# Router with its weights' parts stationary and x1 moving, and the gate bias as two float32r products

## The chip, the cores and the metric

One core of one Trainium2 chip. The metric is the device time of one launch in microseconds (us); the kernel before was run three times, and one further execution was profiled. TensorE's clock has two levels, 1.2 and 2.4 GHz; the profile gives the granted clock of a stretch as a share of the higher one.

## The reference, cut to what matters

A hybrid encoder layer with 768 tokens (256 of a prompt, 512 of a sample) and width 1024. After attention and SSD mixing, an output projection and a layer norm give x1. From x1 come two things that the change touches:

```
aff  = softmax(x1 @ w_router)            # 16 experts; per sequence each expert takes its top 32 / 64 tokens
gate, idx = top_k(aff.T, cap)            # 96 tokens per expert in all
moe  = scatter-add over 16 experts of  down(silu(x1[idx] @ w_gate) * (x1[idx] @ w_up)) * gate
ple  = sigmoid(x1 @ w_ple_gate + b_ple_gate) * (p @ w_ple)
y    = layer_norm(ALPHA * x1 + moe + ple)
```

Everything is float32. Sums that must stay exact to float32 are formed from a high and a low part of each operand, rounded to float32r: high x high, high x low, low x high.

## The kernel before, in words

All five engines run a program written out by hand and meet at semaphores. Tokens stand in NT = 6 tiles of 128; D = 1024 is KD = 8 blocks of 128. The stages up to x1 take some 485 us. What follows around the change, with line numbers of the kernel before:

- **x1.** VectorE's x1_norm(t) (L1313) norms tile t and counts s_x1. TensorE's x1_turn(t) (L1779, transposes at L1787) turns it into PSUM; ScalarE's x1_high(t) copies the high part to xT_r, VectorE's x1_low(t) (L1323, L1327) writes the low part to mix_r and counts s_x1T.
- **Gate units.** ple_units are 12 pairs (half h of 512 columns, tile t), h = 0 first. ple_unit(u) (L1791) computes in one PSUM bank: the bias as one f32 product of a row of ones and a bias row (L1800, bias rows in spare space of qksq and dtw, loaded at L504), then 24 float32r products of 512 columns (L1805 to L1807), and in a second bank p @ w_ple as two f32 products (L1811). Each f32 product of 512 columns stands in the trace as two instructions. It counts s_pg. ScalarE's sigmoid(u) (L948) and VectorE's base(u) (L1349, L1350) turn the pair into ALPHA * x1 + ple, which GpSimd writes to acc_rows (L665). Unit u waits for base(u - 2), because the banks alternate.
- **Router.** router(t) (L1815): for tile t, x1's parts are the stationary operand and the router weights move. Eight products of 32 columns (L1818: x1 high with both weight parts), eight of 16 columns (L1820: x1 low with the high part), per tile; 96 in all, into bank 6, with tokens on the partitions. VectorE adds the parts and forms the softmax with one exponential on ScalarE (L1359 to L1367, L976).
- **Search.** TensorE turns the affinities (L1861), VectorE copies them to gB (L1372) and takes the top 32 and 64 tokens in twelve rounds of max, max_index and match_replace (L1379 to L1381) in gB and bB, with base(2), base(3) and base(4) after every fourth round. s_top follows (L1387). TensorE turns the indices (L1868, L1873), and GpSimd gathers rows of x1.
- **TensorE's order** from 476 us: unit 0, x1_turn(5), router of the six tiles, unit 1, affinity turn, units 2 to 5, wait for s_top, index turns, units 6 to 10, turn of expert 0's rows (L1883), unit 11, then the experts: gate_up (L1905) of 384 products and down (L1917) of 384 products each.
- **SyncE's order** (the only queue of weight loads, and a wait there holds all behind it): at s_o NT the first half of expert 0's gate and up weights (load_gu 0 and 1, L512), at s_pg 6 the second half, at s_top the two broadcasts of ln2's gain and bias into gB and bB (L527, L528; 512 KB each in SBUF), at s_pg 12 expert 0's down weights (load_dn, L515), then each expert's weights as the slots come free (s_ug, s_ud).

Of the kernel before, what the change touches and what calls it, by code (L numbers as in the profile page):

```python
# [28 lines left out]
P = 128  # L29
# [36 lines left out]
def hymba_layer(nc, A, consts, out_prompt, out_sample):  # L66
# [16 lines left out]
    with ctx:  # L83
        def sb(name, shape, dt=F32):
            return ctx.enter_context(nc.sbuf_tensor(name, shape, dt))

        def sem(name):
            return ctx.enter_context(nc.semaphore(name))
# [8 lines left out]
        def over(name, base, skip, shape):  # L97
            return nc.alloc_sbuf_tensor_at(name, shape, F32R, offset=at[base] + 4 * skip).ap()
# [14 lines left out]
        ones = sb("ones", [P, P])  # L113
# [70 lines left out]
        bple = [qksq[0:1, 0:512], dtw[0:1, 0:6, :].rearrange("p r c -> p (r c)")[:, 0:512]]  # L184

# [31 lines left out]
        wr2 = over("wr2", "dtw", 512, [P, KD, 2 * NE])  # L217
# [121 lines left out]
        s_bple = sem("s_bple")  # L339
        s_bn = sem("s_bn")  # L340
# [48 lines left out]
        def gate_bank(u):  # L389
            return 2 * (u % 2)  # L390
# [42 lines left out]
        def _(sp):  # L433
# [69 lines left out]
            for h in range(2):  # L503
                sp.dma_start(bple[h], A["b_ple_gate"][:, h * 512:(h + 1) * 512]).then_inc(s_bple, 16)  # L504
# [212 lines left out]
        def _(act):  # L717
# [7 lines left out]
            def copy(o, i):  # L725
                return nc.scalar.activation(o, i, ACT.Copy)  # L726
# [210 lines left out]
            copy(wr2[:, :, 0:NE], wr[:]).then_inc(s_wrh, 1)  # L937
# [72 lines left out]
        def _(dve):  # L1010
# [300 lines left out]
            nc.vector.tensor_tensor(wr2[:, :, NE:2 * NE], wr[:], wr2[:, :, 0:NE], ALU.subtract).then_inc(s_wrl, 1)  # L1311
# [179 lines left out]
        def _(pe):  # L1491
# [299 lines left out]
            def ple_unit(u):  # L1791
                h, t = ple_units[u]
                if u == 0:
                    pe.wait_ge(s_x1T, NT - 1)
                    pe.wait_ge(s_bple, 32)
                    pe.wait_ge(s_wple, 16)
                if u >= 2:
                    pe.wait_ge(s_base, u - 1)
                b, c = gate_bank(u), p_bank(u)
                nc.tensor.matmul(ps[:, b, :], ones[0:1, :], bple[h], start=True, stop=False)  # L1800
                for k in range(KD):
                    if t == 0 and k % 4 == 0:
                        pe.wait_ge(s_wpl, 2 * h + k // 4 + 1)
                    x_h, x_l = xT_r[:, k, t * P:(t + 1) * P], mix_r[:, t, k * P:(k + 1) * P]
                    nc.tensor.matmul(ps[:, b, :], x_h, wpg_h[h][:, k, :], start=False, stop=False)  # L1805
                    nc.tensor.matmul(ps[:, b, :], x_h, wpg_l[h][:, k, :], start=False, stop=False)  # L1806
                    nc.tensor.matmul(ps[:, b, :], x_l, wpg_h[h][:, k, :], start=False, stop=(k == KD - 1))  # L1807
                if u == 2 * NT - 1:
                    pe.wait_ge(s_base, u)
                for k in range(2):  # L1810
                    last = nc.tensor.matmul(ps[:, c, :], pT[:, k, t * P:(t + 1) * P],  # L1811
                                            wple[:, k, h * 512:(h + 1) * 512], start=(k == 0), stop=(k == 1))
                last.then_inc(s_pg, 1)

            def router(t):  # L1815
                o = ps[:, 6, 2 * NE * t:2 * NE * (t + 1)]
# [47 lines left out]
            for u in range(2, 6):  # L1864
                ple_unit(u)
# [118 lines left out]
```

## Time and profile before

| | us |
|---|---|
| median of 3 runs | 1182.03 (1181.91 to 1183.86) |
| the profiled execution, its own time | 1182.11 |
| its span, first to last instruction | 1180.3 |
| TensorE busy | 1072.2 (91% of the span) |
| VectorE, ScalarE, GpSimd busy | 439.7, 253.0, 287.5 |
| mean granted clock of TensorE | 0.960 |
| moved by DMA | 254.01 MB, 215 GB/s over the span |

The time of the execution is 1.8 us above its span. Busy time of TensorE contains products that wait in its pipeline, so the distance between starts tells the price of a product, not its length. Times of rows count from the start of the span. A bracket at the end of a row of a timeline is the idle time before it and what ended that.

### The profile page before, as it was taken

To read this page: it belongs to the slowest core of one execution; us is meant where nothing else is said; L and a number is where in the kernel's file an instruction comes from. 1 tells how busy PE (TensorE), PEld (TensorE's weight loads), DVE (VectorE), ACT (ScalarE), POOL (GpSimd) and SP (SyncE) were. 2 spreads that over 40 slices of the span, in tenths; PEclk is the share of its full clock that TensorE was granted. 3 is DMA by queue.
4 is the path that set the end of the run, shared out by engine and by line. 5 is a ranking of instruction groups with operands and counts; after the bars stand their busy time and mean duration, and the time that the engine had idled before them with its cause. 6 is when DMAs were issued, how large, how long until landed. Compare 5 with 4: busy or idle time off the path is not lost.

```text
span 1180.3 us, 20730 instructions
## 1 busy us (share of the span) xinstructions
PE 1072.2 (91%) x8811; PEld 611.9 (52%) x8811; DVE 439.7 (37%) x870; ACT 253.0 (21%) x530; POOL 287.5 (24%) x311
## 2 busy tenths in 40 slices
PE   5999778888998899999999999999999999999940
PEld 3568666665655587866643344444443344444420
DVE  5436785457678867656100011111011011111018
ACT  1143334256656621300011000000000000000002
POOL 0006994234545100000100122211122122210134
PEclk9999988979999999789999999999999999999985
DMA  9010200300000620404269999999999999999854
GB/s 337 14 61 11 72 1 1 98 10 0 2 1 1 211 101 36 187 18 158 97 252 406 385 385 386 398 396 386 388 397 392 390 388 387 397 393 404 320 166 176
DMA packets 63119, 254.01 MB, mean 215 GB/s; under 512 B 7384, under 2 KB 15448, under 8 KB 46688
## 3 DMA queue, kind: packets, MB, share of 16 engines
q1 hardware_dynamic: 52544, 234.48, 50.9%
q0 software_dynamic: 10528, 18.88, 6.5%
q8 instruction: 32, 0.52, 0.2%
q14 instruction: 15, 0.12, 0.0%
HBM read 237.62 MB, written 15.73 MB: 215 GB/s over the span
## 4 chain that ended last, share of the span: by engine, by line
PE 72%; DVE 11%; DMA 7%; POOL 6%; ACT 2%; issue 2%; SPq 0%; DVEq 0%; POOLq 0%; ACTq 0%
PE ps L1905 25%; PE ps L1917 12%; PE ps L1563 4%; DMA ring<-in_w_e_up 2%; DMA late<-in_w_e_down 2%; PE ps L1669 2%; PE ps L1684 2%; PE ps L1805 2%; PE ps L1557 2%; PE ps L1807 2%; PE ps L1806 2%; PE ps L1811 2%; PE ps L1883 1%; PE ps L1774 1%; PE ps L1775 1%
## 5 line engine op out<-in xcount | busy, mean ns | idle before, releaser
L1905 PE MATMUL ps<-ring,mix 128*32 128x512 f32 x1536 | 170.7, 592 | 1.1 <-DMA ring<-in_w_e_up 1.1
L1905 PE MATMUL ps<-late,mix 128*32 128x512 f32 x1536 | 171.1, 593 | 0.0
L1408 DVE TENSOR_TENSOR mix<-mix,ps 128x768 f32<-128x768 f32 x16 | 15.3, 954 | 321.6 <-ACT mix L988 321.6
L988 ACT ACTIVATE mix<-ps 128x768 f32<-128x768 f32 x16 | 13.0, 811 | 478.8 <-PE ps L1905 478.8
L1905 PEld LDWEIGHTS ps<-ring,mix 128*32 128x32 f32 x1536 | 49.7, 110 | 116.5 <-issue 113.4
L1905 PEld LDWEIGHTS ps<-late,mix 128*32 128x32 f32 x1536 | 48.2, 110 | 108.7 <-issue 107.8
L1917 PE MATMUL ps<-late,mix 128*32 128x256 f32 x1536 | 86.2, 380 | 2.9 <-DVE mix L1402 2.5
L1917 PE MATMUL ps<-ring,mix 128*32 128x256 f32 x1536 | 85.9, 379 | 1.4 <-DMA ring<-in_w_e_down 1.4
L1415 DVE TENSOR_SCALAR mix<-ps,att 128x256 f32<-128x256 f32 x48 | 20.3, 477 | 162.0 <-PE ps L1917 162.0
L681 POOL DMA_INDIRECT acc_rows<-mix,idx_now x48 | 74.9, 1561 | 20.5 <-POOL idx_now L689 10.7
L1917 PEld LDWEIGHTS ps<-ring,mix 128*32 128x32 f32 x1536 | 49.7, 110 | 34.6 <-DMA ring<-in_w_e_down 1.9
L1917 PEld LDWEIGHTS ps<-late,mix 128*32 128x32 f32 x1536 | 48.9, 110 | 35.2 <-DVE mix L1402 3.0
L686 POOL COPY idx_now<-idxT 96x1 int32 (+1 forms) x14 | 2.5, 181 | 219.2 <-PE ps L1883 219.2
L689 POOL COPY idx_now<-idx 128x3 int32 (+1 forms) x16 | 3.0, 186 | 195.3 <-DVE mix L1415 195.3
L1646 PE MATMUL ps<-xT 128*128 128x512 f32 (+1 forms) x96 | 45.0, 555 | 1.3 <-issue 1.3
L1563 PE MATMUL ps<-ring,xT 128*128 128x512 f32 x96 | 44.9, 623 | 1.2 <-ACT xT L726 1.2
L1537 PE MATMUL ps<-xl,wh 128*128 128x512 f32 (+1 forms) x128 | 44.0, 344 | 0.0
L850 ACT ACTIVATE ring<-ps,att 128x512 f32<-128x512 f32 (+1 forms) x48 | 29.3, 611 | 49.0 <-DVE att L1182 48.8
L1091 DVE SCALAR_TENSOR_TENSOR late<-late,cw 128x770 f32<-128x770 f32 x32 | 39.1, 1226 | 0.9
L1805 PE MATMUL ps<-ring_r,xT_r 128*128 128x512 f32 x96 | 39.3, 409 | 0.0
L1660 PE MATMUL ps<-cst,ring 128*128 128x128 f32 x160 | 27.9, 291 | 11.4 <-DVE gb_in L1190 5.4
L1806 PE MATMUL ps<-late_r,xT_r 128*128 128x512 f32 x96 | 37.9, 395 | 0.0
(289 smaller groups left out, 1812.4 us busy)
## 6 DMA issues: line engine op xcount, KB each, us to landing
late<-in_w_e_gate SPq DMA_DIRECT2D x32, 1024.0 KB, 18.0
late<-in_w_e_up SPq DMA_DIRECT2D x32, 1024.0 KB, 20.0
ring<-in_w_e_gate SPq DMA_DIRECT2D x32, 1024.0 KB, 17.0
ring<-in_w_e_up SPq DMA_DIRECT2D x32, 1024.0 KB, 20.0
late<-in_w_e_down SPq DMA_DIRECT2D x16, 2048.0 KB
ring<-in_w_e_down SPq DMA_DIRECT2D x16, 2048.0 KB
ring<-in_w_in SPq DMA_DIRECT2D x3, 2048.0 KB, 9.0
late<-in_w_ple_gate SPq DMA_DIRECT2D x2, 2048.0 KB, 14.1
```

What stands on the lines that cost most here:

```text
L681: pool.indirect_dma_start(acc_quarters, bass.IndirectOffsetOnAxis(ap=idx_now[:, 1 + i:2 + i], axis=0), ye[:, i, :], None, compute_op=ALU.a ...
L850: nc.scalar.activation(prob[:, u % 4, 0:L], ps[:, u % 3, 0:L], ACT.Exp, bias=att[:, 0, u:u + 1], scale=HD ** -0.5, accum_out=att[:, 1, u:u ...
L1091: ins = nc.vector.scalar_tensor_tensor(conv[:, m, :], u_pad[:, m, j:j + CW], cw[:, m, j:j + 1], conv[:, m, :], ALU.mult, ALU.add)
L1537: nc.tensor.matmul(o, w_h, xl[:, k, a * P:(a + w) * P], start=False, stop=False)
L1557: last = nc.tensor.matmul(bank[:, 0:272], lhs[k], wkv[:, k, :], start=(k == 0), stop=(k == KD - 1))
L1563: last = nc.tensor.matmul(bank, lhs[k], slotk[0][:, k, :], start=(k == 0), stop=(k == KD - 1))
L1646: nc.tensor.matmul(ps[:, u % 3, 0:n * P], qT[:, h % 4, t * P:(t + 1) * P], kz[:, h // 4, a * P:(a + n) * P], start=True, stop=True).then_i ...
L1660: last = nc.tensor.transpose(ps[:, 3, b * P:(b + 1) * P], prob[:, u % 4, b * P:(b + 1) * P], ident)
L1805: nc.tensor.matmul(ps[:, b, :], x_h, wpg_h[h][:, k, :], start=False, stop=False)
L1806: nc.tensor.matmul(ps[:, b, :], x_h, wpg_l[h][:, k, :], start=False, stop=False)
L1905: last = nc.tensor.matmul(ps[32 * j:32 * (j + 1), GU + g, :].rearrange("p (w c) -> p w c", w=2), xeT[:, k, 32 * g:32 * (g + 1)], gu_w[q][: ...
L1917: last = nc.tensor.matmul(ps[32 * j:32 * (j + 1), DN + g, 0:256], src[:, k, 32 * g:32 * (g + 1)], dn_w[d][:, i, 256 * j:256 * (j + 1)], st ...
```

## The change

- The router becomes router(t0, t1, bank): the stationary operand is a 96-column slice of wr2 (block k's high and low parts in its first 32 columns; what follows them is other blocks' or padding, and its output is not read), and x1's high and low parts move, 512 columns for tiles 0 to 3 and 256 columns for tiles 4 and 5. 32 products instead of 96; the logits come with experts on the partitions.
- ScalarE copies the 32 rows of logits to SBUF (gB), TensorE turns them back per tile (six transposes into bank 4), and VectorE reads them as before.
- The bias row is loaded once to partition 32 of gB, split into a high part (ScalarE, into bB) and a low part (VectorE, in place), and added by two float32r products with a row of ones, behind the 24 products instead of ahead of them.
- ple_unit is cut into ple_gate and ple_rest. New order on TensorE: gate of unit 0, x1_turn(5), router in two parts, rest of unit 0, gate of unit 1, logits' turn, rest of unit 1, unit 2, affinity turn, units 3 to 5, wait for s_top and on as before.
- SyncE loads the bias after the last x1 norm; the down weights of expert 0 go ahead of ln2's broadcasts, which now stand behind s_pg 12.

```diff
@@ SyncE
-            for h in range(2):
-                sp.dma_start(bple[h], A["b_ple_gate"][:, h * 512:(h + 1) * 512]).then_inc(s_bple, 16)
...
             load_gu(0, 0)
             load_gu(0, 1)
+            sp.wait_ge(s_x1, NT)
+            sp.dma_start(bple_raw, A["b_ple_gate"]).then_inc(s_bple, 16)
             sp.wait_ge(s_pg, NT)
             load_gu(0, 2)
             load_gu(0, 3)
+            sp.wait_ge(s_pg, 2 * NT)
+            load_dn(0, 0)
+            load_dn(0, 1)
             sp.wait_ge(s_top, 1)
             sp.dma_start(gB[:], bc(A["ln2_g"][0])).then_inc(s_ln2, 16)
             sp.dma_start(bB[:], bc(A["ln2_b"][0])).then_inc(s_ln2, 16)
-            sp.wait_ge(s_pg, 2 * NT)
-            load_dn(0, 0)
-            load_dn(0, 1)
@@ ScalarE
-            copy(wr2[:, :, 0:NE], wr[:]).then_inc(s_wrh, 1)
+            copy(wr2k[:, :, 0, :], wr[:])
+            copy(wr2[:, KD * 2 * NE:], wr[:, 0:4, :].rearrange("p k e -> p (k e)")).then_inc(s_wrh, 1)
...
+            act.wait_ge(s_bple, 16)
+            copy(bple_h, bple_raw).then_inc(s_bplh, 1)
+            act.wait_ge(s_lg, 1)
+            copy(logitsT[:, 0:512], ps[0:2 * NE, 6, :])
+            copy(logitsT[:, 512:T], ps[0:2 * NE, 7, 0:T - 512]).then_inc(s_lgT, 1)
             sigmoid(0)
             wpg_high(1, 0)
             wpg_high(1, 1)
@@ VectorE
+            nc.vector.tensor_copy(ones_r, ones[:])
...
+            dve.wait_ge(s_bplh, 1)
+            nc.vector.tensor_tensor(bple_l, bple_raw, bple_h, ALU.subtract).then_inc(s_bpll, 1)
             base(0)
             wpg_low(1, 0)
             wpg_low(1, 1)
-            dve.wait_ge(s_lg, 1)
-            lg2 = ps[:, 6, 0:NT * 2 * NE].rearrange("p (t w e) -> p t w e", t=NT, w=2)
+            dve.wait_ge(s_lg, 2)
+            lg2 = ps[:, 4, 0:NT * 2 * NE].rearrange("p (t w e) -> p t w e", t=NT, w=2)
@@ TensorE
+            def ple_rest(u):
+                h, t = ple_units[u]
+                if u == 0:
+                    pe.wait_ge(s_bpll, 1)
+                    pe.wait_ge(s_wple, 16)
+                c = slice(h * 512, (h + 1) * 512)
+                nc.tensor.matmul(ps[:, gate_bank(u), :], ones_r[32:33, :], bple_h[:, c], start=False, stop=False)
+                nc.tensor.matmul(ps[:, gate_bank(u), :], ones_r[32:33, :], bple_l[:, c], start=False, stop=True)
...
+            def router(t0, t1, bank):
+                o = ps[0:CAP, bank, 0:(t1 - t0) * P]
                 for k in range(KD):
-                    last = nc.tensor.matmul(o, xT_r[:, k, t * P:(t + 1) * P], wr2[:, k, :], start=(k == 0), stop=False)
-                for k in range(KD):
-                    last = nc.tensor.matmul(o[:, 0:NE], mix_r[:, t, k * P:(k + 1) * P], wr2[:, k, 0:NE], start=False,
-                                            stop=(k == KD - 1))
-                if t == NT - 1:
+                    w = wr2[:, 2 * NE * k:2 * NE * k + CAP]
+                    nc.tensor.matmul(o, w, xT_r[:, k, t0 * P:t1 * P], start=(k == 0), stop=False)
+                    last = nc.tensor.matmul(o, w, mix_r[:, t0:t1, k * P:(k + 1) * P], start=False, stop=(k == KD - 1))
+                if t1 == NT:
                     last.then_inc(s_lg, 1)
...
-            ple_unit(0)
+            ple_gate(0)
             x1_turn(NT - 1)
             pe.wait_ge(s_wrl, 1)
+            router(0, 4, 6)
+            pe.wait_ge(s_x1T, NT)
+            router(4, NT, 7)
+            ple_rest(0)
+            ple_gate(1)
+            pe.wait_ge(s_lgT, 1)
             for t in range(NT):
-                pe.wait_ge(s_x1T, t + 1)
-                router(t)
-            ple_unit(1)
+                last = nc.tensor.transpose(ps[:, 4, t * 2 * NE:(t + 1) * 2 * NE], logitsT[:, t * P:(t + 1) * P],
+                                           ident[0:2 * NE, 0:2 * NE])
+            last.then_inc(s_lg, 1)
+            ple_rest(1)
+            ple_unit(2)
...
-            for u in range(2, 6):
+            for u in range(3, 6):
                 ple_unit(u)
```

## Rows read from the trace of the kernel before

**Rows 1.** Windows, one expert: us, busy of each engine (instructions), PEclk, DMA share, GB/s
```profile
691.00:724.00 33.00, 33.00 (x399) 13.80 (x398) 3.05 (x7) 1.68 (x3) 5.99 (x6) 1.00 1.03 392
```
**Rows 2.** Line 512, loads issued at 606 to 630 us, then at 1020 to 1050 us
```profile
DMA to landing us min/median/max: 11.9/13.7/15.8
...
DMA to landing us min/median/max: 21.3/24.6/28.4
```
**Rows 3.** Timeline of PE, 549 to 602 us: start us, duration us, instruction
```profile
549.16 0.22 PE L1868 MATMUL ps<-cst 16*96 16x16 f32 x1
...
549.83 1.12 PE L1800 MATMUL ps<-dtw,ones 1*128 1x512 f32 x2
...
591.92 1.02 PE L1883 MATMUL ps<-cst,mix 96*128 96x96 f32 x8
...
601.30 1.92 PE L1905 MATMUL ps<-late,mix 128*32 128x512 f32 x16
```
**Rows 4.** Timeline of PE, 476 to 523 us
```profile
476.23 1.12 PE L1800 MATMUL ps<-qksq,ones 1*128 1x512 f32 x2
...
485.01 1.09 PE L1787 MATMUL ps<-cst,xa 128*128 128x128 f32 x8 [0.28 <-DVE xa L1030]
485.86 1.04 PE L1818 MATMUL ps<-wr,xT_r 128*128 128x32 f32 x8
486.75 1.04 PE L1820 MATMUL ps<-wr,mix_r 128*128 128x16 f32 x8
...
504.06 2.07 PE L1800 MATMUL ps<-qksq,ones 1*128 1x512 f32 x2
...
514.68 0.82 PE L1861 MATMUL ps<-cst,rt 128*16 128x128 f32 x6
515.42 1.12 PE L1800 MATMUL ps<-qksq,ones 1*128 1x512 f32 x2
516.48 0.50 PE L1805 MATMUL ps<-ring_r,xT_r 128*128 128x512 f32 x1
...
522.05 1.88 PE L1811 MATMUL ps<-gb_in,kvd 128*128 128x512 f32 x4
```
**Rows 5.** Windows around the fall and the rise of the clock (columns as rows 1)
```profile
488.00:490.00 2.00, 2.00 (x14) 2.00 (x13) 1.34 (x3) 1.99 (x3) 0.00 (x0) 0.61 0.58 229
...
508.00:510.00 2.00, 2.00 (x8) 1.61 (x7) 0.00 (x0) 0.00 (x0) 0.00 (x0) 0.77 0.00 0
```
**Rows 6.** Line 512, the four loads issued at 476.3 to 479.1 us
```profile
DMA to landing us min/median/max: 9.9/10.7/11.6
```
**Rows 7.** Timeline of VectorE and ScalarE, 483 to 488 us
```profile
483.73 1.22 DVE L1030 TENSOR_TENSOR xa<-xa,bB 128x1024 f32<-128x1024 f32 x1
...
486.14 1.08 ACT L726 ACTIVATE xT_r<-ps 128x512 fp32r<-128x512 f32 x2 [4.75 <-PE ps L1787]
```
**Rows 8.** Timeline of VectorE, 516 to 547 us
```profile
516.84 0.94 DVE L1372 COPY gB<-ps 16x768 f32<-16x768 f32 x1
...
524.66 0.69 DVE L1349 TENSOR_TENSOR ssdw<-ssdw,ps 128x512 f32<-128x512 f32 x1 [1.47 <-ACT ssdw L948]
...
546.17 0.18 DVE L1387 TENSOR_SCALAR cst<-cst 16x64 f32<-16x64 f32 x1
```
**Rows 9.** Windows with idle time of PE, and after (columns as rows 1)
```profile
156.00:160.00 4.00, 0.99 (x8) 0.86 (x8) 3.69 (x5) 3.29 (x6) 3.84 (x4) 1.00 0.00 0
168.00:171.00 3.00, 1.28 (x6) 1.12 (x7) 2.96 (x3) 2.95 (x6) 2.92 (x3) 1.00 0.00 0
171.00:175.00 4.00, 3.03 (x8) 1.82 (x6) 3.93 (x5) 1.21 (x1) 3.84 (x4) 0.57 0.00 0
```
**Rows 10.** Line 527, issued at 551.3 us, and windows near it (columns as rows 1)
```profile
DMA to landing us min/median/max: 13.3/13.3/13.3
...
560.00:564.00 4.00, 4.00 (x20) 3.28 (x19) 0.80 (x4) 0.00 (x0) 0.54 (x1) 1.00 1.00 326
564.00:568.00 4.00, 4.00 (x12) 1.85 (x11) 0.56 (x1) 0.60 (x1) 0.00 (x0) 1.00 0.42 166
```

More of the change, by code:

```diff
@@ L112, in hymba_layer @@
         hpar = sb("hpar", [P, 3, 16])
-        ones = sb("ones", [P, P])
+        ones = sb_at("ones", [P, P])
         wr = sb("wr", [P, KD, NE])
@@ L216, in hymba_layer @@
         wpg_raw, wpg_h, wpg_l = [slotk[4], slotk[5]], [ring_r[1], ring_r[2]], [late_r[1], late_r[2]]
-        wr2 = over("wr2", "dtw", 512, [P, KD, 2 * NE])
+        wr2 = over("wr2", "dtw", 0, [P, KD * 2 * NE + 2 * 32])
+        wr2k = wr2[:, 0:KD * 2 * NE].rearrange("p (k w e) -> p k w e", k=KD, w=2)
+        logitsT = gB[0:2 * NE, 0:T]
+        ones_r = over("ones_r", "ones", 0, [P, P])
+        gB_r, bB_r = over("gB_r", "gB", 0, [P, D]), over("bB_r", "bB", 0, [P, D])
+        bple_raw, bple_h, bple_l = gB[32:33, :], bB_r[32:33, :], gB_r[32:33, :]
         HALF_K = [slice(0, 4), slice(4, 8)]
@@ L339, in hymba_layer @@
         s_bple = sem("s_bple")
+        s_bplh = sem("s_bplh")
+        s_bpll = sem("s_bpll")
+        s_lgT = sem("s_lgT")
         s_bn = sem("s_bn")
@@ L1310, in _ @@
             dve.wait_ge(s_wrh, 1)
[L1311 removed]
+            nc.vector.tensor_copy(ones_r, ones[:])
+            nc.vector.tensor_tensor(wr2k[:, :, 1, :], wr[:], wr2k[:, :, 0, :], ALU.subtract).then_inc(s_wrl, 1)
             def x1_norm(t):
@@ L1789, in x1_turn, with ple_gate @@
                 last.then_inc(s_tr, 1)
-            def ple_unit(u):
+            def ple_gate(u):
                 h, t = ple_units[u]
@@ L1794, in ple_unit @@
                     pe.wait_ge(s_x1T, NT - 1)
-                    pe.wait_ge(s_bple, 32)
-                    pe.wait_ge(s_wple, 16)
                 if u >= 2:
                     pe.wait_ge(s_base, u - 1)
-                b, c = gate_bank(u), p_bank(u)
-                nc.tensor.matmul(ps[:, b, :], ones[0:1, :], bple[h], start=True, stop=False)
                 for k in range(KD):
@@ L1803, in ple_unit @@
                         pe.wait_ge(s_wpl, 2 * h + k // 4 + 1)
+                    o = ps[:, gate_bank(u), :]
                     x_h, x_l = xT_r[:, k, t * P:(t + 1) * P], mix_r[:, t, k * P:(k + 1) * P]
-                    nc.tensor.matmul(ps[:, b, :], x_h, wpg_h[h][:, k, :], start=False, stop=False)
-                    nc.tensor.matmul(ps[:, b, :], x_h, wpg_l[h][:, k, :], start=False, stop=False)
-                    nc.tensor.matmul(ps[:, b, :], x_l, wpg_h[h][:, k, :], start=False, stop=(k == KD - 1))
+                    nc.tensor.matmul(o, x_h, wpg_h[h][:, k, :], start=(k == 0), stop=False)
+                    nc.tensor.matmul(o, x_h, wpg_l[h][:, k, :], start=False, stop=False)
+                    nc.tensor.matmul(o, x_l, wpg_h[h][:, k, :], start=False, stop=False)
+            def ple_rest(u):
[6 more added lines that the diff above has]
+                nc.tensor.matmul(ps[:, gate_bank(u), :], ones_r[32:33, :], bple_l[:, c], start=False, stop=True)
                 if u == 2 * NT - 1:
@@ L1810, in ple_unit @@
                 for k in range(2):
-                    last = nc.tensor.matmul(ps[:, c, :], pT[:, k, t * P:(t + 1) * P],
-                                            wple[:, k, h * 512:(h + 1) * 512], start=(k == 0), stop=(k == 1))
+                    last = nc.tensor.matmul(ps[:, p_bank(u), :], pT[:, k, t * P:(t + 1) * P],
+                                            wple[:, k, c], start=(k == 0), stop=(k == 1))
                 last.then_inc(s_pg, 1)
-            def router(t):
-                o = ps[:, 6, 2 * NE * t:2 * NE * (t + 1)]
-                for k in range(KD):
-                    last = nc.tensor.matmul(o, xT_r[:, k, t * P:(t + 1) * P], wr2[:, k, :], start=(k == 0), stop=False)
-                for k in range(KD):
-                    last = nc.tensor.matmul(o[:, 0:NE], mix_r[:, t, k * P:(k + 1) * P], wr2[:, k, 0:NE], start=False,
-                                            stop=(k == KD - 1))
-                if t == NT - 1:
+            def ple_unit(u):
+                ple_gate(u)
+                ple_rest(u)
+            def router(t0, t1, bank):
+                o = ps[0:CAP, bank, 0:(t1 - t0) * P]
+                for k in range(KD):
+                    w = wr2[:, 2 * NE * k:2 * NE * k + CAP]
+                    nc.tensor.matmul(o, w, xT_r[:, k, t0 * P:t1 * P], start=(k == 0), stop=False)
+                    last = nc.tensor.matmul(o, w, mix_r[:, t0:t1, k * P:(k + 1) * P], start=False, stop=(k == KD - 1))
+                if t1 == NT:
                     last.then_inc(s_lg, 1)
```

1 line of the change is left out of this document (removed).

## The prediction, made before the changed kernel was run

> **What bounds the kernel now.** I read the windows of the expert stage first: TensorE is busy in all of the 33 us that one expert takes, and the DMA engines show a share of 1.03 [rows 1]. Two resources are full, so I asked which one falls behind. The time from issue to landing of the expert loads answers that: median 13.7 us for loads issued at 606 to 630 us, 24.6 us at 1020 to 1050 us [rows 2]. The queue grows by some 11 us over 13 experts, so transfers are slightly slower than matmuls. From the first down load at about 601 us on the end is therefore fixed by "start of this stage plus bytes to move". That start hangs on TensorE: SyncE waits for s_pg 12, the end of gate unit 11, and the first expert matmul follows at 601.30 us [rows 3].
>
> So the question is what the change does to TensorE's path from 476 to 601 us, and then what it adds to the DMA queue behind it. TensorE has no gap of note there [rows 3, 4]; its clock has: it falls within 488 to 490 us (mean 0.61) and rises within 508 to 510 us (0.77), so the stretch between, 20.5 us, runs at 1.2 instead of 2.4 GHz [rows 5].
>
> **Up to the affinity turn.** The old router starts at 485.86 and ends at 504.06 us: 96 products in 18.2 us. At full clock eight took 0.89 us, 0.11 each [rows 4], whatever their 16 or 32 columns; at half clock twice that. Unit 1 follows, 10.6 us because half of it is at half clock, then the turn of the affinities (0.74 us) until 515.42 us. That is 29.6 us from router start to turn end.
>
> The new order over the same stretch, at full clock, with 24 products of a gate unit taking 5.57 us, 0.232 each [rows 4]:
> - Router part 1, 16 products of 512 columns: 3.7 us. Part 2, 16 of 256 columns: half the price, 0.116, just over the 0.11 that a new stationary operand costs: 1.9 us. Ends 491.5 us. The Trainium skill, "TensorE: Matmul & The Clock Gate", section "Back-to-back issue gap", gives about 131 ns for a 512-column product in a stream of weight loads and products, and 216 ns isolated. By the first, part 1 would take 2.1 us and the sum would be 1.6 us lower; by this trace's 0.232 us in just such a stream the second is nearer, and I give the first no weight.
> - The rest of unit 0: the two bias products. The f32 bias costs 1.06 us now [rows 4]; no row shows two float32r products of one row. Bounds: twice 0.232 = 0.46 us, or no saving. I take 0.56 (0.46 and a little for the switch of rows), so 0.5 us saved per unit: it is the same instruction kind as the gate's. The P products cost 1.80 us (8.43 for a unit, less 1.06 and 5.57). Together 2.4 us.
> - It must wait for the bias's low part. The bias row is issued after the last x1 norm, whose gap ends at 485.01 us [rows 4], behind four expert loads that land 9.9 to 11.6 us after their issue at 476 to 479 us, the last near 489.0 [rows 6]. Then a copy of 1x1024 on ScalarE (two of 512 columns took 1.08 us) and a subtraction on VectorE (1.22 us) [rows 7]: 491.8 us with hand-overs. TensorE waits some 0.3 us. On ScalarE the logit copies and sigmoid 0 queue behind that copy, on VectorE base 0 and the low parts of the second half's weights; the softmax then ends near 504, while TensorE works until 511. Nobody waits.
> - Gate of unit 1 5.6 us, six turns of the logits 0.74 (as the affinity turn), rest of unit 1 2.4, **unit 2, moved ahead**, 7.9, affinity turn 0.74.
> Sum 25.8 us: the turn ends at 511.7 instead of 515.4 us, 3.7 us earlier although it now has unit 2 ahead of it.
>
> **From the turn to the experts.** Now: 515.42 to 601.30 us, 85.9 us [rows 3, 4]. Units 2 to 5 take 8.43 us each (33.7 us to 549.16) and cover the top-k search. That search runs on VectorE from 516.84 to 546.35 us with 1.47 us of waiting in it, 28.0 us of work with three base steps [rows 8]. It is done 2.8 us before TensorE asks.
> After: only units 3 to 5 are left as cover, 3 x 7.93 = 23.8 us. The search needs 0.3 us of hand-over and 28.0 us of work from the turn's end, so **TensorE now stalls 4.5 us**, part of it ahead of unit 5 (which needs base 3) and the rest at s_top. Then 0.67 us of index turns, units 6 to 10 at 7.93 (39.65; now 42.09), the turn of expert 0's rows 0.95, unit 11 7.93: 77.5 us. Saved: 8.4 us. Together 12.1 us at full clock.
>
> **The clock** takes some back. Without bias and P products, unit 0's gate ends at 481.8 us, 3.2 us ahead of x1; now this gap is 0.28 us [rows 4]. Rows on both sides: 3.01 us idle of the 4 us from 156 us left the clock at 1.00; 1.72 us idle of the 3 us from 168 us were followed by about 3.4 us at half (0.57 over 171 to 175 us) [rows 9]. So it may or may not fall; I think it mostly does, and dense 512-column products then bring it back sooner than the old router did. I take 5 us at half clock, 2.5 us lost (bounds 0 and half of 20.5 us). The stall at s_top with the tiny index products behind it can do the same ahead of unit 6; a fall ahead of unit 5 instead would be covered by the search. I take 1.0 us, between 0 (clock stays, or the search covers it) and 3.4 (7 us at half).
>
> **The DMA queue.** The bias's two old loads of 2 KB, on an idle queue, cost nothing. The two 512 KB broadcasts of ln2 move from an idle queue at 551 us to behind the first down loads, ahead of every load of expert 1. They are then in the stage that the queue bounds, and the price is their time on the queue. By bytes, 1.05 MB at the stage's 392 GB/s [rows 1] are 2.7 us; at the 326 GB/s that a full queue (share 1.00) moved from 560 to 564 us, while they were in it, 3.2 us [rows 10]. The upper end is their landing time of 13.3 us [rows 10]. I take 3.1, near the row in which they ran themselves. Nothing hides it: TensorE's own slack against the queue is used up by the end of the stage.
>
> The other edits (a copy of ones on VectorE, a small second copy of router weights on ScalarE) come before the output products end, while both engines wait for TensorE, and cost nothing; without that cover they would be some 0.5 us.
>
> **Sum**: -12.1 + 2.5 + 1.0 + 3.1 = -5.5 us against the profiled execution's own 1182.11 us (span 1180.3), which stands 0.08 us above the median: 1176.6 us.
>
> **The rivals.**
> A. The clock stays up in both new gaps, as in the first of those rows: -9.0 us, 1173.1; with the bias at its cheap bound and ln2 at 2.7 us, 1171.5. For it: the search has units between its two waits. Against: the second of those rows, where less idle time was enough.
> B. The clock falls at the new gap and stays down through the second router part, bias waits and turns, as it did for 20.5 us, some 15 us, and once more at s_top: 8 to 9 us lost, about 1181. This needs unit 1's dense products not to end it early; now they did, within that unit [rows 5]. A costly bias product ends in the same place: no saving in 8 units on the path is 4 us, 1180.6.
> C. **Slower**: the ln2 broadcasts, all reading one 4 KB row 128 times, hold the queue for most of their 13.3 us landing time when they stand ahead of expert 1. At 13.3 us instead of 3.1 the time is 1186.8. It decides from about 11 us on (3.1 + 5.5 + 2.4). Against: the share of 0.42 over 564 to 568 us shows the queue empty soon after [rows 10].
> D. The change doesn't do what it says: the wide router products run as full f32 (0.90 us for a P product) instead of at the gate's price. The tiles are float32r views as in the gate, so I hold it for unlikely; with 0.9 and 0.45 us per product the router costs 21.6 us, 1192.
>
> **How the numbers follow.** Forecast 0.48, A 0.20, B 0.20, C 0.07, D 0.05. A measurement of this kernel tells about 0.2%, 2.4 us, from no change: faster means below 1179.7. The forecast's own range is 1174 to 1180, nearly all faster; B lies mostly within the bound; C and D are slower, but for part of B that spills over. Faster 0.72, same 0.17, slower 0.11. The range takes in A's low bound and B: 1171.5 to 1182.0; above it lie C and D.
>
> **What would show it.** In the profile after: router products in two groups of about 3.7 and 1.9 us (up to twice that at half clock); a gap of about 3 us ahead of 485 us; gate units at 7.9 us; an idle TensorE ahead of unit 5 and ahead of the index turns, 4 to 5 us together, released by VectorE; first expert matmul near 592.7 us (589 with the clock up); landing of expert 1's first loads some 3 us longer. Wrong would be: a unit still at 8.4 us, no stall at s_top, the first expert matmul after 597 us, or a stage from there to the end that differs from 580 us by other than the ln2 loads' 3 us.

## The result, and the profile after

The changed kernel takes **1174.45 us** (median of 4 runs, 1173.55 to 1174.80) against 1181.97 us before (4 runs beside it): the ratio is 0.9935, 95% interval 0.9919 to 0.9951. It is faster by 7.5 us (0.65%); 5.5 us were forecast. A second measurement, beside 11 runs of the kernel before, gave 1174.14 us and 0.9932 [0.9916, 0.9949].

The profiled execution took 1173.55 us, its span 1171.6 us; so it is 0.9 us under the median, and 8.6 us under the profiled execution of the kernel before. Line numbers below are those of the changed kernel. First the timeline of TensorE after the change, answering to [rows 4]:

```profile
485.19 1.71 PE L1798 MATMUL ps<-cst,xa 128*128 128x128 f32 x8 [3.11 <-DVE xa L1038]
486.55 0.78 PE L1840 MATMUL ps<-xT_r,wr 128*96 128x512 f32 x1
...
491.43 0.28 PE L1840 MATMUL ps<-xT_r,wr 128*96 128x256 f32 x1
...
493.41 0.50 PE L1823 MATMUL ps<-bB_r,ones_r 1*128 1x512 f32 x1
493.75 0.39 PE L1824 MATMUL ps<-gB_r,ones_r 1*128 1x512 f32 x1
494.07 1.99 PE L1828 MATMUL ps<-gb_in,kvd 128*128 128x512 f32 x4
...
501.60 0.50 PE L1823 MATMUL ps<-bB_r,ones_r 1*128 1x512 f32 x1
...
512.14 0.82 PE L1889 MATMUL ps<-cst,rt 128*16 128x128 f32 x6
```

The gap of 0.28 us ahead of x1's last turn has become 3.11 us. The router's first part takes 4.88 us (486.55 to 491.43), its second 1.98 us: 6.9 us instead of 18.2. The two bias products take 0.66 us together (493.41 to 494.07) instead of 1.06. From the bias of unit 0 to the bias of unit 1 it is 8.19 us (493.41 to 501.60), with the six turns of the logits in it. Bias and P products end the unit, and six turns of the affinities start at 512.14 us, 2.5 us earlier than before, although unit 2 now stands ahead of them.

The clock (columns as in [rows 1]), answering to [rows 5]:

```profile
484.00:486.00 2.00, 0.81 (x5) 0.81 (x6) 1.13 (x1) 0.00 (x0) 0.53 (x1) 0.88 1.00 422
486.00:488.00 2.00, 2.00 (x9) 1.56 (x8) 0.00 (x0) 1.06 (x2) 0.00 (x0) 0.50 1.02 418
488.00:490.00 2.00, 2.00 (x8) 1.39 (x7) 1.63 (x3) 1.09 (x2) 0.00 (x0) 0.77 0.63 252
490.00:492.00 2.00, 2.00 (x12) 1.53 (x11) 0.87 (x1) 0.00 (x0) 0.00 (x0) 1.00 0.05 20
```

It falls right behind the gap and is back within 488 to 490 us. By the means (0.12, 0.50 and 0.23 short of 1.00, over 2 us each, doubled) that is 3.4 us at half clock, where it was 20.5 us.

The search and what follows it, answering to [rows 3] and [rows 8], on TensorE and then on VectorE:

```profile
530.80 0.50 PE L1813 MATMUL ps<-ring_r,xT_r 128*128 128x512 f32 x1 [1.62 <-DVE cst L1359]
541.13 0.22 PE L1896 MATMUL ps<-cst 16*96 16x16 f32 x1 [2.03 <-DVE cst L1398]
547.49 0.50 PE L1823 MATMUL ps<-bB_r,ones_r 1*128 1x512 f32 x1
...
555.53 0.50 PE L1823 MATMUL ps<-bB_r,ones_r 1*128 1x512 f32 x1
...
582.14 1.02 PE L1911 MATMUL ps<-cst,mix 96*128 96x96 f32 x8
...
591.18 1.06 PE L1933 MATMUL ps<-late,mix 128*32 128x512 f32 x8
```
```profile
512.99 0.94 DVE L1383 COPY gB<-ps 16x768 f32<-16x768 f32 x1 [5.12 <-PE ps L1889]
...
540.90 0.18 DVE L1398 TENSOR_SCALAR cst<-cst 16x64 f32<-16x64 f32 x1
```

TensorE now stalls for 1.62 us ahead of unit 5 (released by base 3) and 2.03 us at s_top: 3.65 us, both released by VectorE, whose search runs 28.1 us without a wait. A gate unit takes 8.04 us (547.49 to 555.53) instead of 8.43. The first expert matmul comes at 591.18 instead of 601.30 us.

In the expert stage, windows of the same 33 us, then the landing times of loads of line 512 issued at 595 to 620 and at 1010 to 1040 us, answering to [rows 1, 2]:

```profile
691.00:724.00 33.00, 33.00 (x402) 13.88 (x398) 3.15 (x6) 1.68 (x3) 6.00 (x6) 1.00 1.03 395
```
```profile
DMA to landing us min/median/max: 14.3/16.1/18.0
...
DMA to landing us min/median/max: 21.0/24.3/27.9
```

Loads of expert 1 land after 16.1 instead of 13.7 us: the two broadcasts stand ahead of them. How the stage keeps its pace shows in the turns of an expert's rows (L1911), one per expert, and in TensorE's waits from 950 to 1075 us:

```profile
933.68 1.13 PE L1911 MATMUL ps<-cst,mix 96*128 96x96 f32 x8
966.78 1.13 PE L1911 MATMUL ps<-cst,mix 96*128 96x96 f32 x8
1000.62 1.13 PE L1911 MATMUL ps<-cst,mix 96*128 96x96 f32 x8
1034.95 1.13 PE L1911 MATMUL ps<-cst,mix 96*128 96x96 f32 x8
```
```profile
PE ps L1933 <- DMA ring<-in_w_e_up: 2.1, 3, 1.0
```

From the third turn up to 966.78 us an expert takes 33.10 us, before the change and after it: there TensorE sets the pace, while the queue falls behind. Only the last experts wait for their up weights, three times and 2.1 us in all; two of them show here with 33.84 and 34.33 us.

**A ruler.** Across the 13 profiles of this study the start of the last operation of x1's norm lies anywhere from 482.09 to 484.65 us, though nothing ahead of it was changed on purpose but small copies. TensorE's clock early in the execution goes with it. The windows of 120 to 300 us in the profiles of e3, of the changed kernel and of e8, in which that operation starts at 482.56, 483.91 and 484.65 us:

```profile
120.00:300.00 180.00, 144.66 (x704) 111.14 (x703) 115.59 (x241) 83.46 (x198) 101.12 (x115) 0.92 0.09 30
...
120.00:300.00 180.00, 147.41 (x706) 113.34 (x704) 114.90 (x238) 82.72 (x194) 100.60 (x115) 0.91 0.10 30
...
120.00:300.00 180.00, 148.72 (x705) 115.05 (x704) 114.74 (x237) 82.84 (x194) 100.74 (x114) 0.90 0.09 30
```

The four profiles with a mean clock of 0.92 there (e1, e3, e6, e10) have the operation at 482.1 to 482.8 us; of the eight with 0.91, six have it at 483.7 to 484.6 us, and e7 and e5 at 484.31 and 482.36 us. The medians move likewise: of the six runs of e11, the changed kernel again, two with a mean clock of 0.970 and 0.971 over the whole execution took 1171.9 us, four with 0.965 and 0.966 took 1174.1 to 1174.9 us. So medians of 4 to 6 runs can differ by up to 2 us without an edit. What makes the clock fall more or less often in those early stages stays open.

So I compare two stretches: from that start to the index turns (the path of router, gates and search), and from the index turns to the last expert matmul (gates 6 to 11 and the experts).

| kernel | x1 to index turns | index turns to last matmul | median, us |
|---|---|---|---|
| before | 65.43 | 587.7 | 1181.97 |
| changed | 57.22 | 586.8 | 1174.45 |
| changed, again | 57.24 | 587.2 | 1174.14 |

The first stretch repeats to 0.02 us, the second to half a us. The change gains 8.2 us in the first and, with cheaper gates against the ln2 loads, 0.5 to 0.9 us in the second. That goes with the 8.6 us between the two profiled executions; the medians differ by 7.5 us.

### The profile page after: what moved, and what is told of

Its sections match the earlier page's. It is cut to its first block, busy times and chain, and to the rows that moved or that the text cites. A ratio compares the mean times of both kernels' runs of the same rounds, so it can differ in the third digit from the quotient of the medians.

```text
span 1171.6 us, 20620 instructions
## 1 busy us (share of the span) xinstructions
PE 1057.4 (90%) x8753; PEld 600.2 (51%) x8753; DVE 441.1 (38%) x872; ACT 255.4 (22%) x534; POOL 287.7 (25%) x311
## 4 chain that ended last, share of the span: by engine, by line
PE 67%; DVE 13%; DMA 9%; POOL 6%; issue 2%; ACT 2%; SPq 0%; DVEq 0%; POOLq 0%; ACTq 0%
PE ps L1933 24%; PE ps L1945 11%; DMA ring<-in_w_e_up 7%; PE ps L1574 4%; PE ps L1680 2%; PE ps L1695 2%; PE ps L1568 2%; PE ps L1828 1%; PE ps L1785 1%; PE ps L1787 1%; PE ps L1786 1%; PE ps L1813 1%; PE ps L1814 1%; PE ps L1815 1%; DVE xT L1467 1%
## 5 line engine op out<-in xcount | busy, mean ns | idle before, releaser
L1419 DVE TENSOR_TENSOR mix<-mix,ps 128x768 f32<-128x768 f32 x16 | 15.3, 954 | 323.0 <-ACT mix L996 323.0
L683 POOL DMA_INDIRECT acc_rows<-mix,idx_now x48 | 75.0, 1562 | 20.5 <-POOL idx_now L691 10.7
```

Of the source, the lines that this page charges most:

```text
L683: pool.indirect_dma_start(acc_quarters, bass.IndirectOffsetOnAxis(ap=idx_now[:, 1 + i:2 + i], axis=0), ye[:, i, :], None, compute_op=ALU.a ...
```

## The experiments

Each is the changed kernel with the edit shown. Its ratio is to the kernel before, measured beside it. "Under" and "above the changed kernel" compare with its first median, 1174.45 us, where nothing else is said, and carry the uncertainty of up to 2 us told above; the first stretch is free of it.

**e1: the f32 bias back.**

```diff
-nc.tensor.matmul(..., ones_r[32:33, :], bple_h[:, c], start=False, stop=False)
-nc.tensor.matmul(..., ones_r[32:33, :], bple_l[:, c], start=False, stop=True)
+nc.tensor.matmul(..., ones[32:33, :], bple_raw[:, c], start=False, stop=True)
```

> The changed kernel with one part undone: the gate bias is again one f32 product of a row of ones and the bias row (still behind the 24 gate products, still loaded after the last x1 norm); the copy to a high part on ScalarE and the subtraction on VectorE are gone. Theory (TensorE's path sets the start of the expert stage, and units 3 to 5 are hidden by the search): the bias costs about 1.05 us per unit instead of 0.66 us, 0.39 us more. Of twelve units nine are on the path (units 0 to 2 and 6 to 11), so the first expert matmul comes at 591.2 + 3.5 = 594.7 us and the time is 1174.45 + 3.5 = 1178.0 us; the two stalls of the search shrink from 3.65 to about 2.5 us together. Rival (the bias is paid in all twelve units, the search hides nothing): +4.7 us, 1179.1. Rival (the float32r form saves nothing at this width): 1174.5.

Measured: 1177.29 us (0.9958 [0.9942, 0.9975]), 2.8 us above the changed kernel, between the three expectations and nearest to the first; its four runs (1176.1 to 1178.9 us) don't separate the first from the second, the waits below do. Its units and its clock behind the index turns, from the timeline and the windows:

```profile
549.18 1.12 PE L1818 MATMUL ps<-gB,ones 1*128 1x512 f32 x2
...
557.63 1.12 PE L1818 MATMUL ps<-gB,ones 1*128 1x512 f32 x2
```
```profile
542.00:546.00 4.00, 4.00 (x11) 3.13 (x12) 0.50 (x1) 0.00 (x0) 0.54 (x1) 0.57 0.99 393
```

A unit costs 8.45 us again, 0.4 us more than with float32r products, and the first stretch is 58.42 us, 1.20 us longer: three units' bias, as only units 0 to 2 stand ahead of the search. The waits shrink from 3.65 to 2.56 us, so units 3 to 5 are indeed covered. In this profile the clock fell behind the wait at s_top (0.57 over 542 to 546 us, 3.4 us at half); in the changed kernel's own two profiles it did not. It is the slowest of the four runs, 1178.86 us.

**e2: the old router back**, with unit 2 still ahead of the affinity turn.

```diff
-router(0, 4, 6)
-pe.wait_ge(s_x1T, NT)
-router(4, NT, 7)
+for t in range(NT):
+    pe.wait_ge(s_x1T, t + 1)
+    router(t)
...
-act.wait_ge(s_lg, 1)
-copy(logitsT[:, 0:512], ps[0:2 * NE, 6, :])
-copy(logitsT[:, 512:T], ps[0:2 * NE, 7, 0:T - 512]).then_inc(s_lgT, 1)
...
-    last = nc.tensor.transpose(ps[:, 4, t * 2 * NE:(t + 1) * 2 * NE], logitsT[:, t * P:(t + 1) * P],
```

router(t) and wr2 have their old form again, and VectorE reads the logits from bank 6.

> The changed kernel with the other part undone: the router as before the change (x1's parts stationary, 96 products per run of six tiles, logits with tokens on the partitions, no copy of logits and no turn back), in the place where the new router stands; the bias as two float32r products, unit 2 ahead of the affinity turn, and ln2's loads behind the down loads stay. Theory (the router was dear because of its 96 changes of the stationary operand and because the clock fell under it): router 17 to 19 us instead of 6.9 us, unit 1's first part at half clock again, less 0.2 us of logit turn; first expert matmul at 601 to 604 us, time 1185 to 1187 us, slower than the kernel before, since the search's stall and the ln2 loads are still paid. Rival (the half clock came from the old order and its f32 bias, not from the router's small products): the router costs 10.8 us at full clock, +4 us, 1178.5.

Measured: 1189.71 us (1.0067 [1.0050, 1.0083]), 15.3 us above the changed kernel and 3 us more than the theory's upper end. From its timeline, the start of the router and of the bias behind it, then its windows:

```profile
487.04 1.87 PE L1836 MATMUL ps<-wr,xT_r 128*128 128x32 f32 x8
...
507.60 0.79 PE L1819 MATMUL ps<-bB_r,ones_r 1*128 1x512 f32 x1
```
```profile
486.00:488.00 2.00, 2.00 (x12) 2.00 (x10) 0.00 (x0) 0.58 (x2) 0.20 (x1) 0.50 1.05 436
...
512.00:514.00 2.00, 2.00 (x8) 1.36 (x7) 0.77 (x2) 1.41 (x2) 0.00 (x0) 0.80 0.00 0
```

Here the clock is down when the router starts, behind the gap (3.15 us), and stays down through it and into the next gate, from 485.5 to 512.8 us: 27.3 us instead of the 20.5 us before the change. The router's 96 products take 20.6 us, all at half clock. In this order the new router is worth more than the whole change. The miss of the theory is that it took the old router at its old price, of which the first part ran at full clock, and the old length of half clock with it.

**e8: the bias part alone**, e2 and in addition unit 2 behind the affinity turn, as before the change; against e2:

```diff
 ple_rest(1)
-ple_unit(2)
...
-for u in range(3, 6):
+for u in range(2, 6):
```

> Of the change only the bias part and what it forces: old router in its old form and unit 2 behind the affinity turn as before, bias as two float32r products behind the gate's, ln2's broadcasts behind the down loads. Theory (the float32r bias saves 0.39 us per unit on TensorE, 4.7 us, while the gap ahead of 485 us costs 3.1 us, the half clock that begins in it and lasts through the router 3 to 4 us more, and ln2's loads 3.5 us): slower than the kernel before, 1185 to 1187 us. Rival (the bias part pays for itself): 1179 to 1181 us.

Measured: 1184.94 us (1.0033 [1.0021, 1.0044]): slower than before, at the lower end of what was expected. Split off from the router, the bias part loses: its row must wait for x1's gain and bias rows to be free, which opens the gap, costs clock under the old router, and pushes the ln2 loads into the expert stage. The 4.7 us that it saves on products by the theory don't pay that; the parts were not measured one by one here. e5 below has the order of e8 with the new router, 1169.20 us: with unit 2 behind the affinity turn the router is worth 15.7 us, with unit 2 ahead of it 15.3 us (e2).

**e3: the ln2 loads behind the last down load.**

```diff
-sp.wait_ge(s_top, 1)
-sp.dma_start(gB[:], bc(A["ln2_g"][0])).then_inc(s_ln2, 16)
-sp.dma_start(bB[:], bc(A["ln2_b"][0])).then_inc(s_ln2, 16)
...
     load_dn(NE - 1, d)
+sp.wait_ge(s_top, 1)
+sp.dma_start(gB[:], bc(A["ln2_g"][0])).then_inc(s_ln2, 16)
+sp.dma_start(bB[:], bc(A["ln2_b"][0])).then_inc(s_ln2, 16)
```

> The changed kernel with ln2's two broadcasts issued after the last down load of the expert stage instead of ahead of expert 1's loads; nothing else. Theory (the DMA queue bounds the expert stage, so 1 MB ahead of it costs its time on the queue): 2.5 to 3.2 us faster, 1171.5 us. Rival (TensorE bounds most of the stage, and the stage's end hangs on the last down load's own latency): within 0.8 us of 1174.45. Second rival (the late loads then delay the closing layer norm, which waits for them): slower than 1174.45 by up to 10 us.

Measured: 1170.90 us (0.9914 [0.9898, 0.9931]), 3.5 us under the changed kernel and 3.2 us under its second measurement. Landing of line 512's loads issued at 596 to 620 us, and TensorE's waits from 950 to 1075 us:

```profile
DMA to landing us min/median/max: 10.2/13.5/15.8
```
```profile
PE ps L1933 <- DMA ring<-in_w_e_up: 0.8, 1, 0.8
```

Median 13.5 instead of 16.1 us, and 0.8 instead of 2.1 us of waits. The first stretch is unchanged (57.26 us), the second 583.5 instead of 587 us. No wait of the closing norm for the late loads stands in the profile. The steadiest measure runs from the first expert matmul to the end of the span: 578.2, 578.0 and 577.4 us in the three profiles with late loads (e3, e7, e10) against 580.3 to 580.8 us in seven with early ones (the changed kernel twice, e2, e5, e6, e8, e9; e1 has 581.8). The broadcasts cost 2.7 us between the means, 2.1 to 3.4 us between single profiles.

So both theories were right in part. TensorE sets the pace of most experts, as the rival said; but the queue never makes up for the megabyte, and the last experts pay for it.

**e4: the ln2 loads twice.**

```diff
 sp.dma_start(bB[:], bc(A["ln2_b"][0])).then_inc(s_ln2, 16)
+sp.wait_ge(s_ln2, 32)
+sp.dma_start(gB[:], bc(A["ln2_g"][0])).then_inc(s_ln2, 16)
+sp.dma_start(bB[:], bc(A["ln2_b"][0])).then_inc(s_ln2, 16)
```

> The changed kernel with ln2's two broadcasts issued a second time, when the first pair has landed, still early in the expert stage (1 MB more on the queue, nobody computes with it); SyncE waits for the first pair to land before that, which also holds back the loads of expert 1 behind it. Theory (queue bound): +3 us for the megabyte and up to some us more for the loads held back, 1178 us or above. Rival (TensorE bound): the queue has room, within 0.8 us of 1174.45.

Measured: 1180.99 us (0.9996 [0.9982, 1.0009]), 6.5 us above the changed kernel, with ten runs from 1178.65 to 1184.68 us. Slow enough for the theory, but for another reason: the hold of SyncE. Expert 1's loads leave at 610.6 instead of 596.6 us, and TensorE waits for them, with the clock at half behind that wait:

```profile
622.23 6.98 PE L1936 MATMUL ps<-late,mix 128*32 128x512 f32 x48 [7.17 <-DMA late<-in_w_e_up]
```
```profile
618.00:626.00 8.00, 3.77 (x20) 1.04 (x24) 0.00 (x0) 0.00 (x0) 0.00 (x0) 0.57 1.01 365
```

By the mean of 0.57 the clock is at half for some 6.9 us. The wait and half of that are 10.6 us; the stage of this profile is 590.2 us, 9.8 us longer than the changed kernel's. So nothing is left that would be the second megabyte's, and e4 can't tell a price per megabyte. That rests on e3, e7 and e10.

**e5: unit 2 behind the affinity turn.**

```diff
 ple_rest(1)
-ple_unit(2)
...
-for u in range(3, 6):
+for u in range(2, 6):
```

> The changed kernel with unit 2 moved back behind the affinity turn, as before the change. Theory (the search of 28.3 us needs four gate units of 8.04 us as cover, and has three): TensorE waits about 1 us for the softmax ahead of the affinity turn, the turn ends near 506 us instead of 513, units 2 to 5 run to 538.3 us without a wait ahead of unit 5 or at s_top, so the index turns begin 2.8 us earlier than the 541.1 us of the changed kernel, and the time is 1171.7 us. Rival (the 3.65 us of waiting there are not on the path, the DMA queue is): 1174.45 us, no change. Rival (the softmax comes so late that unit 2 ahead of the turn was needed): slower than 1174.45.

Measured: 1169.20 us (0.9899 [0.9883, 0.9916]). Its timeline of TensorE, with VectorE's last norm operation at 482.36 us:

```profile
503.59 0.82 PE L1888 MATMUL ps<-cst,rt 128*16 128x128 f32 x6 [1.12 <-DVE rt L1378]
...
536.53 0.22 PE L1895 MATMUL ps<-cst 16*96 16x16 f32 x1
```

A wait of 1.12 us for the softmax, none at s_top: 54.17 us for the first stretch, 3.05 us less than the changed kernel, as expected. The median moved by 5.2 us. The second stretch (587.3 us) doesn't hold the other 2 us. The early x1 does in the profiles: 1169.03 against 1173.55 us are 4.5 us, of which 3.05 lie in the first stretch and 1.55 ahead of it (482.36 against 483.91 us). The mean clock of its four runs is 0.968 and 0.969, that of the changed kernel's four 0.965 to 0.967.

**e6: the gap filled.**

```diff
 ple_gate(0)
-x1_turn(NT - 1)
 pe.wait_ge(s_wrl, 1)
+pe.wait_ge(s_res, NT)
 router(0, 4, 6)
+x1_turn(NT - 1)
+ple_gate(1)
 pe.wait_ge(s_x1T, NT)
 router(4, NT, 7)
 ple_rest(0)
-ple_gate(1)
```

> The changed kernel with router part 1 (tiles 0 to 3) ahead of x1's last turn and the gate of unit 1 behind that turn, ahead of router part 2, so that TensorE has work in the gap of 3.1 us ahead of 485 us and while tile 5's parts are copied. Unit 2 stays whole ahead of the affinity turn. Theory (gap and the half clock that it brings lie on the path): 3.1 us of gap and 1.7 us of half clock go, the affinity turn comes 4.3 to 4.8 us earlier, the search with its waits moves along, first expert matmul at 586.6 us, time 1169.9 us; no fall of the clock near 485 us. Rival (the bias row or the softmax on VectorE ends last then, since their times don't move): 1.5 to 2.5 us gained only, 1172.3.

Measured: 1170.07 us (0.9911 [0.9895, 0.9928]). Timeline of TensorE, x1's last norm operation at 482.09 us:

```profile
483.78 1.03 PE L1798 MATMUL ps<-cst,xa 128*128 128x128 f32 x8
...
505.33 0.82 PE L1890 MATMUL ps<-cst,rt 128*16 128x128 f32 x6
...
534.59 0.22 PE L1897 MATMUL ps<-cst 16*96 16x16 f32 x1 [2.03 <-DVE cst L1398]
```
```profile
476.00:1110.00 634.00, 623.97 (x6632) 287.39 (x6630) 104.41 (x206) 47.71 (x74) 94.31 (x103) 1.00 0.89 341
```

No gap, and the granted clock does not fall from 476 us up to the tail of the expert stage at 1110 us. The first stretch is 52.50 us, 4.72 us less: the theory's 4.3 to 4.8.

**e9: fillers in the gap.** Twelve float32r products of 512 columns, whose result nobody reads, ahead of x1's last turn.

```diff
 ple_gate(0)
+pe.wait_ge(s_wrl, 1)
+pe.wait_ge(s_res, NT)
+for k in range(12):
+    nc.tensor.matmul(ps[0:CAP, 7, :], wr2[:, 0:CAP], xT_r[:, k % KD, 0:512], start=True, stop=True)
 x1_turn(NT - 1)
```

> The changed kernel with 12 float32r products of 512 columns, whose result nobody reads, in the gap of 3.1 us ahead of x1's last turn; all that is read is computed as before. Theory (the clock falls because of the gap, and half a clock for 3.4 us costs 1.7 us of path): no fall of the clock near 485 us, the path from the start of x1's last norm operation to the index turns 55.5 instead of 57.2 us, time 1.7 us less than the changed kernel. Rival (the turn of 128x128 blocks or the following waits bring the fall, not the gap): the clock falls all the same, no gain. Second rival (the fillers delay the turn): up to 1 us slower.

Measured: 1172.24 us (0.9913 [0.9895, 0.9931]), 1.9 us under the second measurement of the changed kernel, made beside it. Its windows and, from its timeline, x1's last turn and the index turns (x1's last norm operation: 484.46 us):

```profile
540.00:544.00 4.00, 3.93 (x57) 3.23 (x58) 1.30 (x3) 0.00 (x0) 1.00 (x2) 0.57 0.99 371
484.00:488.00 4.00, 3.54 (x20) 2.53 (x19) 1.66 (x3) 1.09 (x2) 0.53 (x1) 1.00 1.01 420
```
```profile
485.74 1.09 PE L1798 MATMUL ps<-cst,xa 128*128 128x128 f32 x8 [0.46 <-DVE xa L1038]
...
540.07 0.22 PE L1900 MATMUL ps<-cst 16*96 16x16 f32 x1 [2.02 <-DVE cst L1398]
```

x1's last turn starts 1.28 us behind the start of the norm operation, as in the changed kernel, so only the idle time ahead of it went (0.46 instead of 3.11 us). The clock stays at 1.00 from 484 to 488 us, and the first stretch is 55.61 us, 1.61 us less. So the gap brought the fall, and the fall cost half of its 3.4 us, apart from the gap's own 3.1 (e6 less e9). In this profile, as in e1, the clock fell at the index turns instead (0.57 over 540 to 544 us).

**e7: gap filled, ln2 loads last, and the affinity turn between gate and rest of unit 2.** The edits of e6 and e3, and:

```diff
 ple_rest(1)
-ple_unit(2)
+ple_gate(2)
...
+ple_rest(2)
 for u in range(3, 6):
```

> All that the runs so far and the two above point to, in one kernel: order with the gap filled, the affinity turn between gate and rest of unit 2 (the softmax lands near 505.5 us, so the search starts 2.5 us earlier than behind the whole unit), and ln2's broadcasts behind the last down load. Theory (the three parts are on one path and add up): 4.5 for the gap, 0.9 for the earlier search, 3.5 for ln2 as measured: 1165.5 us. Rival (parts overlap, as the DMA queue gets its loads earlier but no faster): at most the ln2 gain and half of the rest, 1168 us or more.

Measured: 1166.21 us (0.9871 [0.9854, 0.9887]). x1's last norm operation at 484.31 us:

```profile
506.30 0.82 PE L1890 MATMUL ps<-cst,rt 128*16 128x128 f32 x6 [1.11 <-DVE rt L1378]
...
536.86 0.22 PE L1898 MATMUL ps<-cst 16*96 16x16 f32 x1 [2.03 <-DVE cst L1398]
```

The first stretch is 52.55 us, no better than e6: moving the turn ahead gained nothing. The turn waits 1.11 us for the softmax, which on VectorE stands behind the low parts of the second half's gate weights, 4.5 us, and base 1 behind that. The ln2 part is there in full (second stretch 584.7 us, e6 587.5).

**e10: the same with that wait taken away.** Gap filled and ln2 loads last as in e7. The two low parts go to GpSimd, ScalarE does the exponential and sigmoid 1 ahead of their high parts, and unit 2 stands whole behind the turn.

```diff
-sigmoid(0)
-wpg_high(1, 0)
-wpg_high(1, 1)
-act.wait_ge(s_lgd, 1)
-... ACT.Exp ...
-sigmoid(1)
+sigmoid(0)
+act.wait_ge(s_lgd, 1)
+... ACT.Exp ...
+sigmoid(1)
+wpg_high(1, 0)
+wpg_high(1, 1)
@@ VectorE
 base(0)
-wpg_low(1, 0)
-wpg_low(1, 1)
@@ GpSimd
+if u == 1:
+    for q in range(2):
+        pool.wait_ge(s_wph, 2 + q + 1)
+        nc.gpsimd.tensor_tensor(wpg_l[1][:, HALF_K[q], :], wpg_raw[1][:, HALF_K[q], :],
+                                wpg_h[1][:, HALF_K[q], :], ALU.subtract).then_inc(s_wpl, 1)
```

> As the combined kernel (gap filled, ln2 behind the last down load), with the new last wait ahead of the search taken away: the low parts of the second half's gate weights are formed on GpSimd instead of VectorE, ScalarE does the exponential and sigmoid 1 ahead of their high parts, and unit 2 stands whole behind the affinity turn. Theory (in the combined kernel the search waits for 4.5 us of low parts on VectorE ahead of the softmax): affinity turn some 4 us earlier, search covered by units 2 to 5, index turns 50.2 us behind the start of x1's last norm operation instead of 52.6 us, time 2.4 us under the combined kernel, 1163.8 us. Rival (GpSimd takes over 10 us per low part, or slows VectorE's search beside it): unit 6 waits for the low parts or the search takes over 30 us, 1166 us or more. Rival (the DMA queue takes the gain back): 1165.5 us.

Measured: **1162.95 us** (0.9845 [0.9829, 0.9862]), the fastest, 18.9 us under the kernel before. Timelines, x1's last norm operation at 482.22 us:

```profile
499.17 0.82 PE L1892 MATMUL ps<-cst,rt 128*16 128x128 f32 x6 [1.57 <-DVE rt L1381]
...
532.54 0.22 PE L1899 MATMUL ps<-cst 16*96 16x16 f32 x1 [0.38 <-DVE cst L1401]
```
```profile
502.52 9.13 POOL L672 TENSOR_TENSOR late_r<-late,ring_r 128x2048 fp32r<-128x2048 f32 x2
```

The first stretch is 50.32 us (expected 50.2). Search and cover are now equal, with 0.38 us of waiting left; a wait of 1.57 us for the softmax remains ahead of the affinity turn. GpSimd needs 4.6 us per low part where VectorE needed 2.3, but has only the writes of acc_rows to issue beside them.

**e11** was the changed kernel again:

> The changed kernel itself once more, beside the two kernels below. Every theory expects 1174.5 us within 0.2%. The start of the last operation of x1's norm (line 1038) has moved between 482.1 and 484.7 us in the profiles so far although nothing ahead of it was changed; this run shows how far the medians move with it.

It gave 1174.14 us with x1's operation at 484.56 us in its profile, against 483.91 us in the first; its six runs span 1171.9 to 1174.9 us, in the two groups told above.

## Why the prediction was right

The mechanism was in the main the one named: TensorE's path sets the start of the expert stage, and the stage's length changes by little. The terms:

- **Router**: 3.7 and 1.9 us were forecast at full clock. Measured 4.88 us with 3.4 us of half clock in and ahead of it, and 1.98 us. e2 shows it as the part that carries the change.
- **Bias**: 0.56 us per unit forecast, 0.66 measured; 0.4 instead of 0.5 us saved per unit, and a unit costs 8.04 instead of 7.93 us. Nine units are on the path (three ahead of the search, six behind it), so 1.0 us less is gained; rival B counted eight.
- **Wait for the bias row**: forecast 0.3 us, with the row ready at 491.8 us. VectorE's subtraction started at 489.66 us and took 1.22 us, so it was ready at 490.9, and the router ended only at 493.3 us: no wait.
- **Turns of the logits**: forecast 0.74 us, like the affinity turn. They took some 0.15 us (8.19 us from bias to bias against a unit's 8.04).
- **Search without cover**: 4.5 us of stall forecast, in two places, released by VectorE; 3.65 us measured in just these places. e5 shows that it was on the path: moving unit 2 back gains 3.05 us there.
- **The clock**: forecast 5 us at half behind the gap; it was 3.4 us, 1.6 to 1.7 us lost instead of 2.5 (e9). At s_top 1.0 us was taken on; the changed kernel's two profiles show no fall, e1's and e9's do. These two terms were 1.8 us too dear.
- **ln2's loads**: 3.1 us forecast, 2.7 us measured (e3, e7, e10), in the range of 2.1 to 3.4. TensorE's slack against the queue is used up by the end of the stage, as forecast; but up to some 967 us TensorE sets the pace, where the prediction took the queue to bound the stage from its first down load on.

The sum was forecast for an execution like the profiled one: 1176.6 us. That one took 1173.55 us, 3.05 us less (the median is 2.15 us under the forecast). Half of this lies ahead of the first expert matmul, 591.18 instead of 592.7 us. There the clock 1.8 us, the logits' turns 0.6 and the bias row 0.3 were too dear, the gate units 1.0 too cheap. (The prediction's own terms up to the affinity turn add up to 25.7 us, not 25.8.) The other half lies behind it: from the first expert matmul to the end of the span it was 579.0 us before and is 580.4 and 580.6 us in the changed kernel's two profiles. The forecast was 3.1 us more, and the prediction named any other difference as a sign of being wrong; on this point it was. The loads cost what was forecast within the noise, so some other 1.2 us of the stage went away with the change. Only one profile shows the stage before, and which part it is stays open. That 5.5 us came as near as it did to 7.5 us is in part luck, since misses of both signs met in the sum.

Of the rivals, A (the clock stays up) came half true, at s_top only; its 1173.1 us was nearer to the median (1.35 us) than the forecast (2.15 us), though it had the first gap wrong. B's long stretch of half clock did come, but only with the old router behind the gap (e2, e8); with the new router's products behind it the clock was back after 3.4 us. C fell with e3: the broadcasts cost about what their bytes cost (2.7 us at the stage's 392 GB/s), not their landing time of 14.6 and 15.8 us. D fell with the router's rows.

The Trainium skill's 131 ns for a 512-column product in a stream ("TensorE: Matmul & The Clock Gate", "Back-to-back issue gap") is not met here: part 1 of the router ran at 0.232 us per product once the clock was back.

## What to carry to other kernels

Of a small product with a large stationary operand, let the small side be stationary: 96 products at 0.11 to 0.21 us each became 32, and behind the same gap the clock was back in 3.4 us instead of 27.3 us. When a step gets cheaper, look for what it had covered: here the gain uncovered a search on VectorE, a gap ahead of a norm, and 4.5 us of preparation in front of a softmax. Closing these takes 6.9 us from the first stretch (57.22 to 50.32 us, e10), where the change itself gained 8.2 us; with ln2's loads put last (2.7 us) that is 9.6 of the 11.5 us between the two medians, and x1 starts 1.7 us earlier in e10's profile than in the changed kernel's. A load that moves into a stage whose queue falls behind costs about its bytes, even if nobody needs it for 500 us and most of the stage seems bound by another engine; put it at the stage's end. A stage that is full on two resources needs both measures: the pace told that TensorE sets it for most experts, the landing times told who pays at the end.

## What was not expected

An execution's start of the same operation, 480 us into the program, varies by 2.6 us between profiles of kernels that are alike up to there, and with it the clock between 120 and 300 us; medians of 4 to 6 runs move by up to 2 us with it. A gap of 3.1 us of TensorE was followed by half clock every time (in all eight profiles that have it). A wait of 2.0 us at s_top with small products behind it was followed by it in one profile of eight (e9), and one of 1.6 us also (e1), in nearly the same code. And e4, meant to measure a megabyte, measured a hold of the queue.
